# Two-block steps and half query projections in windowed attention, a fused maximum, and three gate projections moved into the memory heads

## The reference, cut to what matters

```python
h = rmsnorm(x); z = h @ W_in       # pool | q (1024) | k | v | qm (512) | gate logits (3 x 1024)
# window attention: 16 heads of 64, blocks of 128 queries, each sees its own and the previous key block
s = q . kband * HEAD_DIM ** -0.5 ; s = where(mask, s, NEG)
m = maximum(max(s), sink); p = exp(s - m); p = p / (sum(p) + exp(sink - m)); o = p @ vband
# memory attention: 4 heads of 128 into 256 memory tokens, softmax without sink
g = sigmoid(gate_logits)
merged = g0 * (y_pool @ w_pool_out) + g1 * (y_swa @ w_swa_out) + g2 * (y_mem @ w_mem_out)
x = x + merged @ w_out
```

## Time and profile before

| | us |
|---|---|
| median of 3 runs | 1755.6 (1749.4 to 1761.51) |
| the profiled execution, its own time | 1749.71 |
| span of that execution in the trace | 1747.7 |
| PE busy in the span | 1687.8 (97%) |
| DVE busy | 1214.4 (69%) |
| POOL busy | 899.4 (51%) |
| ACT busy | 740.6 (42%) |

### The profile page before, as it was taken

How to read it: one execution, slowest core, us unless ns; L and a number is a source line. 1 busy time by engine, 2 the same in 40 slices (tenths; PEclk the granted TensorE clock), 3 DMA queues, 4 the chain that set the end, 5 groups by cost and what they waited for, 6 DMA issues and landing times.

```text
span 1747.7 us, 26632 instructions
## 1 busy us (share of the span) xinstructions
PE 1687.8 (97%) x9077; PEld 1482.8 (85%) x9077; DVE 1214.4 (69%) x2190; ACT 740.6 (42%) x1105; POOL 899.4 (51%) x573
## 2 busy tenths in 40 slices
PE   6989999999999999999899999998999999999997
PEld 5766778888878899999899999998888888888886
DVE  6578612121136699999698888732988888888888
ACT  5467742232242233333366666633333333333333
POOL 7531224444433358998788989885233233333320
PEclk9999999999999999999999999999999999999999
DMA  6211112222322237899779999999999999999993
GB/s 249 89 50 48 37 48 97 96 96 96 108 73 84 84 134 284 298 311 317 263 252 339 360 331 356 338 393 337 401 364 355 378 366 342 378 359 347 378 361 121
DMA packets 127105, 424.76 MB, mean 243 GB/s; under 512 B 13264, under 2 KB 29648, under 8 KB 124880
## 3 DMA queue, kind: packets, MB, share of 16 engines
q1 hardware_dynamic: 80688, 264.28, 42.2%
q0 software_dynamic: 36864, 134.23, 20.9%
q10 hardware_dynamic: 9504, 25.71, 3.7%
HBM read 371.74 MB, written 52.43 MB: 243 GB/s over the span
## 4 chain that ended last, share of the span: by engine, by line
PE 79%; DVE 14%; ACT 3%; DVEq 1%; issue 1%; DMA 1%; POOL 0%; SPq 0%; ACTq 0%
PE bank L821 30%; PE both L511 15%; PE bank L522 12%; PE bank L511 7%; PE bank L526 6%; PE bank L804 2%; DVE rows L1390 2%; PE bank L721 2%; DVE chosen L1472 2%; DVE cand L1414 1%; ACT swp L931 1%; PE both L631 1%; DVE chosen L1466 1%; DVE chosen L1460 1%; PE bank L761 1%
## 5 line engine op out<-in xcount | busy, mean ns | idle before, releaser
L464 POOL TENSOR_TENSOR w_lo<-raw,w_hi 128x1024 fp32r<-128x1024 f32 (+1 forms) x302 | 596.8, 1988 | 434.7 <-ACT w_hi L869 433.8
L869 ACT ACTIVATE w_hi<-raw 128x1024 fp32r<-128x1024 f32 x346 | 367.0, 1061 | 869.5 <-PE bank L821 316.5
L485 POOL DMA_INDIRECT rows<-stream,idx x256 | 298.6, 1167 | 369.6 <-DVE both L1578 309.2
L522 PE MATMUL bank<-hT_hi,w_hi 128*128 128x384 f32 x1024 | 348.1, 340 | 4.5 <-ACT abuf L1068 4.5
L522 PE MATMUL bank<-hT_lo,w_hi 128*128 128x384 f32 x1024 | 343.6, 336 | 0.0
L821 PE MATMUL bank<-w_hi,wT_hi 128*128 128x512 f32 x768 | 196.3, 391 | 5.1 <-ACT wT_hi L1107 5.1
L526 PE MATMUL bank<-hT_hi,w_lo 128*128 128x384 f32 x1024 | 198.4, 334 | 0.8 <-POOL w_lo L464 0.8
L522 PEld LDWEIGHTS bank<-hT_hi,w_hi 128*128 128x128 f32 x1024 | 193.5, 189 | 4.8 <-issue 4.8
L821 PE MATMUL bank<-w_hi,wT_lo 128*128 128x512 f32 x768 | 195.5, 390 | 0.0
L821 PE MATMUL bank<-w_lo,wT_hi 128*128 128x512 f32 x768 | 195.2, 389 | 0.0
L1563 DVE TENSOR_TENSOR w_lo<-raw,w_hi 128x1024 fp32r<-128x1024 f32 x128 | 156.8, 1225 | 53.6 <-ACT w_hi L869 53.2
(11 more groups left out here) (257 smaller groups left out, 2256.4 us busy)
## 6 DMA issues: line engine op xcount, KB each, us to landing
raw<-stream SPq DMA_DIRECT2D x346, 512.0 KB, 5.2
a_rows<-abuf ACTq DMA_DIRECT2D x64, 384.0 KB, 5.9
g_rows<-gstage SPq DMA_DIRECT2D x32, 768.0 KB, 8.7
g_in<-g_rows SPq DMA_DIRECT2D x16, 1536.0 KB, 10.2
a_in<-a_rows SPq DMA_DIRECT2D x64, 384.0 KB, 6.4
rows<-stream,idx POOLq DMA_INDIRECT x256, 7.2
x_sb<-x SPq DMA_DIRECT2D x4, 512.0 KB, 8.4
out<-x_sb SPq DMA_DIRECT2D x4, 512.0 KB, 3.0
```

Source lines behind the costliest of these rows:

```text
L464: last = pool.tensor_tensor(w_lo[:, k % 2, cols], raw[:, k % RAW, cols], w_hi[:, k % 2, cols].bitcast(f32), ALU.subtract)
L485: pool.indirect_dma_start(rows[:, g % SLOTS, :], None, table, bass.IndirectOffsetOnAxis(idx[:, g // HK, g % HK:g % HK + 1], 0)).then_inc(g ...
L522: pe.matmul(dst, w_hi[:, slot, k * P:(k + 1) * P], hT[low][:, k, DENSE], start=(k == 0 and low == 0), stop=False)
L869: act.activation(w_hi[:, base % 2, :], raw[:, slot, :], ACT.Copy).then_inc(hi_ready, 1)
```

## The change

- **PE, windowed heads.** `window_values` works in steps of two blocks. It now also carries the query projection, cut into two halves of 12 matmuls, and the order in iteration u is: scores(u), transposes of blocks 0 and 1, first half of query u+2, values 0 and 1, transposes 2 and 3, second half, values 2 and 3. The first half waits for `proj_read` (DVE has read the query before out of bank 0) and `swapped` (ACT has copied it).
- **DVE, windowed heads.** Four mask additions, four maxima and the step with the sinks become eight `tensor_tensor_reduce` of 256 columns: one instruction adds the mask, scales, writes the scores and takes the maximum with the sink as its start. It is followed in the program by the small instruction that writes the accumulator. The read of bank 0 stands behind the first two. Sums and scaling go in halves of two blocks, each behind its own `expd`, and `outputs_low` stands last.
- **ACT, windowed heads.** The `split` moves behind the first two copies of probabilities, the sink's exponential ahead of the others; the copies of blocks 2 and 3 stand between the exponentials of blocks 1 and 2; the swap copies of the next query stand behind all exponentials, and `outputs_high` last. The exponentials have no scale any more.
- **Memory heads.** Query chunk 24 goes in halves into `window_values(7)`, chunk 25 between the transposes and the values of head 0, and the three gate projections of output block 0 between those of heads 1, 2 and 3. Gates use banks 0, 2, 3, branches 1, 5, 4, and the window branch comes first (the two chunks change places in the stream). The PE loop over blocks starts with the second pair; ACT's loop is written out.

```diff
+GATE_BANKS, BRANCH_BANKS = (0, 2, 3), (1, 5, 4)
+            def query_part(n, rn, swaps, k0, k1):
+                if k0 == 0:
+                    chunk(n)
+                    pe.wait_ge(proj_read, rn)
+                    if swaps is not None:
+                        pe.wait_ge(swapped, swaps)
+                for k in range(k0, k1):
+                    for wi, (w, low) in enumerate(passes):
+                        last = pe.matmul(bank[0][:, :], ...)
+                if k1 == KC:
+                    last.then_inc(chunk_used, 1)
+            def window_values(u, *query):
...
+                for j in range(2):
+                    turn_block(2 * j)
+                    turn_block(2 * j + 1)
+                    query_part(*query, 4 * j, 4 * j + 4)
+                    if j == 0 and u >= 1:
+                        pe.wait_ge(y_lo, 4 + u)
+                    value_block(2 * j)
+                    last = value_block(2 * j + 1)
                 last.then_inc(attended, 1)
...
+                elif u == 1:
+                    memory_values(0, lambda: query_part(S_QM + 3, R_QM + 3, None, 0, KC))
+                elif u == 2:
+                    pe.wait_ge(proj_read, R_QM + 4)
+                    memory_values(1, lambda: branch_gate(0, 0, 0))
                 else:
+                    pe.wait_ge(score_read, 44)
+                    memory_values(2, lambda: branch_gate(0, 0, 1))
+            memory_values(3, lambda: branch_gate(0, 0, 2))
...
+            next_q(0)
             for u in range(8):
-                next_q(u)
                 if u >= 1:
-                    turn_probs(TT, 4 * (u - 1))
-                    outputs_high(8 + u - 1, u)
+                    turn_probs(2, 4 * (u - 1))
+                split(S_Q + u + 3)
                 act.wait_ge(capped, u + 1)
+                act.activation(sexp[:, :], sdiff[:, :], ACT.Exp)
...
+                    if n == 1 and u >= 1:
+                        turn_probs(TT, 4 * (u - 1), first_n=2)
+                next_q(u + 1)
+                if u >= 1:
+                    outputs_high(8 + u - 1, u)
...
+                    for n in (2 * j, 2 * j + 1):
+                        last = dve.tensor_tensor_reduce(
+                            pr[:, n, h, :], bank[2 + 2 * h + j][:, ...],
+                            mask[:, min(n, 1), :], HEAD ** -0.5, sinks[...], ALU.add, ALU.max,
+                            mcap[:, 2 * n + h:2 * n + h + 1])
+                    last.then_inc(score_read, 1)
+                    if b == 0 and u < 7:
+                        rotate_bank(*turned_q)
```

More of the change, by code:

```diff
@@ new lines, in branches @@
+            def branches(c0, dc, before=None):
+                n = S_GATE + GATE_CHUNKS * dc + 3
+                if before is None:
+                    pe.wait_ge(branch_read, c0 * 3 + (3 * dc + 3))
+                else:
+                    before()
+                chunk(c0 * GATE_CHUNKS + n)
+                product(bank[5][:, :], n % 2, yT, 0, 8, 8)
+                chunk(c0 * GATE_CHUNKS + (n + 1))
+                if dc == 0:
+                    pe.wait_ge(y_lo, 16)
+                product(bank[1][:, :], (n + 1) % 2, yT, 0, 4, 0, used=False)
+                product(bank[4][:, :], (n + 1) % 2, yT, 4, 8, 4)
@@ new lines, in gates_and_branches @@
+            def gates_and_branches(c0, dc):
+                for b in range(3):
+                    if b == 0:
+                        pe.wait_ge(gated, c0 * 3 + (3 * dc + 3))
+                    branch_gate(c0, dc, b)
+                branches(c0, dc)
+            branches(0, 0, before=lambda: pe.wait_ge(score_read, 48))
+            gates_and_branches(0, 1)
+            with pe.Fori(2, KC - 2 + 1, 2) as c0:
+                for dc in range(2):
+                    gates_and_branches(c0, dc)
@@ L973, in _, with next_q @@
             mix_high(3)
-            def next_q(n, ahead=True):
-                if ahead:
-                    split(S_Q + n + 3)
+            def next_q(n):
                 if n + 1 < 8:
```

185 lines of the change are left out of this document (81 added, 104 removed).

## The result

Over six runs each the changed kernel takes 1740.7 us in the median (1739.3 to 1743.2) and the kernel before 1754.6 (1749.4 to 1761.5): a ratio of 0.9926, with a 95% interval of 0.9911 to 0.9942, 13.9 us less. The profiled executions lie closer: 1743.2 us with a span of 1741.2 against 1749.7 with 1747.7, 6.5 us apart. The first is the slowest of its six, the second nearly as fast as the fastest of its own. So there are two questions: where the trace's 6.5 us come from, and why the medians are twice as far apart.

What follows compares the result with a forecast made beforehand. PE, busy 97% of the span, was taken as the bound, with its idle and low-clock time to be won. Savings of 3.9 (start), 3.8 (windowed) and 5.5 (memory heads) made 13.2 us: 1742.5 against 1755.6, range 1730 to 1758.

Steps and rivals of the forecast that it cites:

- two rings of nearly the same length: Windowed heads before the change: PE with ACT and DVE with ACT, about 13.3 us each; shortening one alone gains little.
- the floor of 11.9 us of PE's own work: Windowed iteration: PE's work without waits, including about 0.2 for cutting the projection in two.
- The new ring, 9.9 + 8t: Windowed iteration through `yT_hi`, `yT_lo`, eight fused instructions of step t, exponentials and swap copies; 12.9 us predicted.
- PE will wait some 1.0 us in each iteration: Windowed heads: PE waits about 1 us at `swapped`, ahead of the first half projection, no longer at ACT's copies.
- t = 0.37: Windowed heads: assumed step in us of one fused maximum on DVE, between bounds of 0.34 and 0.61.
- The rival's t of 0.64: Dear fused instruction in windowed heads, from the skill's half-throughput rule for two non-bf16 SBUF sources: 1757 us; rival's chance 0.10.
- (a): Start, up to the scores of head pair 2: 3.9 us saved, the middle of 2.4 to 5.4.
- (b): Windowed heads, scores of pair 2 to pair 7: 66.30 us becomes 62.5, two iterations at 11.9 and three at 12.9.
- (c): Memory heads, pair 7 to the gates of output block 1: gates and chunk 25 fill PE's waits, 5.5 us saved.
- The profiled execution as the reference: Whole kernel: 1749.7 becomes 1736.5 profiled; lying 5.9 below the runs' median, it gives 1742.5 against 1755.6.
- only the memory part holds: Rival: low clock in windowed heads or a 13.3 us ring; (b) 0 to 1, 7.5 saved in all, 1748; chance 0.25.
- The open rings: Rival: `outputs_low` does not bind or DVE overlaps more; windowed iterations take 11.9, 18 us saved, 1737; chance 0.13.

Runs made afterwards that it cites:

- the fastest kernel: Changed kernel with `outputs_low` one pair later, right behind DVE's read of bank 0: median 1733.8 us, ratio 0.9868 against the kernel before.
- The run that cuts the ring: Changed kernel with `outputs_low` one pair later, behind the maxima: median 1735.0 us, ratio 0.9884 against the kernel before.
- the unfused kernel: Changed kernel with the old four additions, four maxima and sinks step instead of eight fused instructions: median 1750.9 us, ratio 0.9957 against the kernel before.

## Why the prediction was right, and where it was not

The time was forecast at 1742.5 and is 1740.7; the saving of 13.2 us against the runs shown before is 13.9 by the medians. But the sum was made against the profiled execution, and there it should have been 13.2 and was 6.5. Much of the agreement is luck: the windowed stretch lost where it should have gained, the memory heads gained more than their bound, and a gain in the medians that the prediction did not know of filled the rest.

- **PE's idle time is what can be won; two rings of nearly the same length.** Right. The fused maxima alone shorten DVE's ring by 1.9 a pair, the split behind the swap shortens its scaling, and both leave 13.2 us. But the floor of 11.9 us of PE's own work is wrong: it is 11.3 in the new order (one iteration of the fastest kernel took 11.43). The prediction charged 0.2 for the cut, and the new order gave 0.5 back.
- **The new ring, 9.9 + 8t.** Right in its course through `yT_hi`, `yT_lo`, fused maxima and exponentials, and in its size. With the measured step of 0.40 it is 13.1, and `yT_lo` comes 13.01 us apart where nothing disturbs it. It comes 13.47 and 13.48 apart where the negation of the maxima takes 0.64 or 0.65 us and not 0.17, beside POOL's `w_lo`, and 14.39 apart behind the projection at the lower clock, where ACT's copies wait 1.14 us for PE's late transposes. The run that cuts the ring gave 6 us, the one that puts t at some 0.6 again cost 7.1 (74.28 - 67.22). The prediction's price, 0.8 us an iteration for each 0.1 of t, would give five iterations with t 0.2 larger 8.
- **"PE will wait some 1.0 us in each iteration [...] at `swapped`."** Wrong in place and size. PE waits 1.52 to 2.16 us from pair 2 on, for `proj_read`: the sum has the read of bank 0 among the fused instructions, but not that PE's half stands behind it. In those five iterations the swap was done 2.9 us before the half began.
- **t = 0.37.** Measured 0.403, inside the bounds of 0.34 and 0.61. The term was 0.03 too small, 0.3 an iteration. The Trainium skill's figure in "VectorE: DVE Perf Modes", the section on the TRN2 errata, gave 3.1 us for eight, and the trace has 8 x 0.40 = 3.2: the Trainium skill was nearer than my step. The rival's t of 0.64 did not come; as one of the two sources is in PSUM, that says nothing on two in SBUF.
- **(a) the start, 3.9 saved, by bounds 2.4 to 5.4.** 2.5, near the lower bound. The lower clock did come back, as the bound allowed: 4.58 us for a half projection where others take 2.97, so 1.6, about what "I take the middle" had for it (1.5). The step that failed is the half's start. Counted from the first scores it comes 1.9 us later than the 110.7 of the text: the exponentials began 1.0 later than said, and the half waits for the read of bank 0, 0.8 behind the swap. PE's shorter work gives 0.6 back.
- **(b) the windowed stretch, 3.8 saved.** Wrong in sign: 0.9 lost, 4.7 from the forecast. "The new ring needs about two iterations until it comes last; I count two at 11.9" failed: the first was already 12.83, which with a ring of 13.0 in the second makes 2.0, and 0.3 more in the three at 12.9. The held negation, no term of the sum, adds 0.47 twice, together 0.9. The lower clock adds 1.4 to the ring (14.39 against 13.01). These are 4.6 of the 4.7. The lower clock behind pair 2 was on the list of what would show the prediction wrong; its price was put on a rival and not in the sum.
- **(c) the memory heads, 5.5 saved, by bounds 1.5 to 6.5.** 7.5, outside the bounds. The gates fill the gaps wholly: PE is idle 0.2 us of 42.4, at full clock. Idle time fell by 4.6 - 0.2 and the clock gives about 1.5 (0.97 over 51.8 us before); 1.6 of PE's busy time is left. The sum took that busy time as unchanged; why it fell is open, though PE's work fell in the windowed heads as well.
- **Behind it nothing changes.** It holds as far as the traces can say. Of the 8.6 us at block 1 some 2 are given back between the experts and the value products, but the unedited kernel loses 1.9 in the same place from its first profile to its second, and the second profile of the changed kernel has the short way again.
- **The profiled execution as the reference.** This is the step that hid the misses. The text took its 5.9 us below the median for a constant offset. It was a good case among the runs of that kernel, in two ways: POOL's `w_lo` lay beside only the end of the scaling, and the way through memory was short. The changed kernel has its scaling behind the exponentials, in fours, and `w_lo` beside the fused maxima, which keep their 0.40 there; in both profiles no group of four takes more than 1.15. That fits its runs, which lie within 3.9 us where those of before lie 12 apart. The run with the split behind the swap shows that the collision makes the upper tail of before. That it is the whole difference between the gain of the medians (13.9) and that of the traces (6.5) isn't shown: taking the collision away gained 1.9 of these 7.4, on a chip where before stood low, and the scatter of the way through memory, 1.9 us between two profiles of before, is a second source.

Of the rivals, "only the memory part holds" was nearest in the trace (its (b) of 0 to 1 saved against 0.9 lost), the forecast in time. The open rings came only with another edit: `outputs_low` one pair later, which is the edge that this rival named.

## What to carry to other kernels

Write each new order down as a ring (who waits for whom until the first engine waits again) and ask which edge can be one pair later for nothing: here a single late `outputs_low` was worth another 7 us in the windowed stretch (67.22 to 60.09) over the change as made. Before a sum is made against one profile, compare its time with the spread of the runs; a kernel that spreads by 12 us may have two courses, and a change's gain can lie in leaving the bad one. When PE is to wait 2 to 3 us between pieces of work, price the half projection behind it at the lower clock as well (4.5 us against 3.0), and ask whether PE is on the ring: where it had slack, three such spells cost nothing. Read a ring's period from an engine that is on it.

## What the hardware showed that I had not expected

- **Some of VectorE's operations within SBUF are held up by GpSimd's.** Eight scaling operations of 256 columns take 2.19 us alone, 2.66 where their last 0.9 us lie beside `w_lo`, and 4.07 where all 3.11 us of `w_lo` lie beside them; a negation of eight columns takes 0.65 to 0.76 instead of 0.17. The fused instruction, one source in PSUM, stays at 0.40, and four maxima of the unfused kernel at 2.46, though `w_lo` ran beside them (158.83 to 161.62, in the row shown above). The Trainium skill has this in "SBUF — State Buffer", the section on the two separate sides of SBUF: GpSimd and a VectorE operation that uses both ports share one pair under an exclusive lock. The trace agrees that they get in each other's way (the eight lose 1.88 us beside the 3.11 of `w_lo`); that the form of operation decides it is seen here from these four only.
- **A kernel can hold itself in such a collision.** The delay moves both instructions alike, so they meet again in the next iteration, four times in a row at 14.56 or 14.57 us. What starts it in one execution and not in another is open.
- **The clock falls behind short waits, and the length of the wait doesn't tell which.** In the changed kernel it was 0.50 behind waits of 2.90 and 2.16 us; behind one of 2.14, two iterations later, the matmuls kept their 0.39 and the clock its 1.00. In its second profile it was 0.50 behind 2.13 and 1.00 behind 2.17, and in the unfused kernel 0.50 behind 1.97 and 1.00 behind 1.94 and 1.95. The same iteration was hit in both profiles of the changed kernel and in the windowed part alone.
